# First projection to pooling as one stage, and attention units ordered by query tile

## The reference

```python
h = rmsnorm(x, norm1_w)
p = h @ w_in                                   # 1024 -> 20 blocks of 128 channels
p_rw = p + mu[0] * (prev - p) + mu[1] * (nxt - p)   # token shift, 16 of the blocks
r, k, v, wd, ad, gd = split(p_rw)
kk = heads(k * k_k); kk = kk / max(sqrt(sum(kk * kk)), 1e-12)
g = sigmoid(gd) @ g_up
for d in range(2):                             # both directions of time
    wlog = -softplus(-(w0[d] + tanh(wd[d]) @ w_up[d])) - 0.5
    decay = exp(-exp(wlog)); a = sigmoid(a0[d] + ad[d] @ a_up[d])
    kd = k * (1 + (a - 1) * k_a)
    o += wkv7_scan(r, decay, kd, v, kk, a, reverse=(d == 1))
    bonus += sum(r * kd * r_k) * v
y_pool = multiscale_pool(p_pool, pool_w, pool_scale)   # windows 2, 4, 8, 16
...
s = einsum('bnqhd,bnkhd->bnhqk', q, k) * 64 ** -0.5 + bias   # 8 heads of mixer A, 8 of B
o = einsum('bnhqk,bnkhd->bnqhd', softmax(s), v)
```

## Time and profile before

| | |
|---|---|
| median of 3 runs | 3314.09 us (3310.55 to 3316.93) |
| the profiled execution | 3311.4 us, of which the span of instructions 3309.2 us |
| TensorE busy | 2833.8 us, 86% |
| VectorE busy | 1845.0 us, 56% |
| ScalarE busy | 1138.4 us, 34% |
| GpSimd busy | 733.5 us, 22% |
| mean granted TensorE clock | 0.949 |

### The profile page before, as it was taken

One profiled execution on the slowest core, in us unless ns is written; L12 is line 12 of the kernel. 1 busy time (PEld: TensorE's weight loads), 2 busy tenths in 40 slices (PEclk: granted clock), 3 DMA queues, 4 the chain that ended last, 5 costly groups with the idle time before them and its releaser, 6 DMA issues. The chain is left out here.

```text
span 3309.2 us, 44276 instructions
## 1 busy us (share of the span) xinstructions
PE 2833.8 (86%) x15630; PEld 1842.2 (56%) x15630; DVE 1845.0 (56%) x3559; ACT 1138.4 (34%) x2659; POOL 733.5 (22%) x594
## 2 busy tenths in 40 slices
PE   8839996987778787877887787998989999999988
PEld 6509995763223233322332224887866776778876
DVE  6673346576676666666664545444256643464422
ACT  3422322224344343434343343222125444332211
POOL 0030000025444554545455551000010000000000
PEclk9859998999999999999999998999999999999999
DMA  3111002349999999999999994323221111232231
GB/s 127 43 60 35 3 3 72 99 179 420 404 405 399 420 415 416 401 420 419 415 407 420 420 421 191 95 94 116 71 96 58 52 58 45 83 96 95 89 123 43
DMA packets 114869, 680.51 MB, mean 206 GB/s; under 512 B 12584, under 2 KB 16552, under 8 KB 46632
## 3 DMA queue, kind: packets, MB, share of 16 engines
q0 software_dynamic: 73728, 536.90, 39.4%
q1 hardware_dynamic: 41000, 141.68, 13.1%
HBM read 673.29 MB, written 7.86 MB: 206 GB/s over the span
## 5 line engine op out<-in xcount | busy, mean ns | idle before, releaser
L1384 PE MATMUL expert_total<-uv_rows,h 128*128 128x512 f32 x2048 | 1009.1, 633 | 268.4 <-ACT h L1479 262.9
L1663 DVE CUSTOM_DVE_ANT_0 uv_rows<-uv_rows,h_tok 128x1024 f32<-128x1024 f32 x512 | 621.6, 1225 | 482.6 <-DMA uv_rows<-in_peer_uv,expert_ids 479.8
L1384 PEld LDWEIGHTS expert_total<-uv_rows,h 128*128 128x128 f32 x2048 | 380.1, 198 | 893.6 <-issue 545.4
L1325 POOL DMA_INDIRECT uv_rows<-in_peer_uv,expert_ids x512 | 647.9, 1265 | 627.3 <-PE expert_total L1384 522.0
L1474 ACT ACTIVATE expert_acts<-expert_dots 128x1 f32<-128x1 f32 x512 | 103.7, 203 | 682.4 <-DVE expert_dots L1663 678.0
L261 PE MATMUL ffn_in_out<-ffn_h_hi,ffn_in_w_hi 128*128 128x512 f32 x704 | 281.3, 400 | 14.9 <-DVE ffn_in_w_lo L346 14.9
L263 PE MATMUL ffn_in_out<-ffn_h_hi,ffn_in_w_lo 128*128 128x512 f32 x704 | 279.8, 397 | 0.0
L262 PE MATMUL ffn_in_out<-ffn_h_lo,ffn_in_w_hi 128*128 128x512 f32 x704 | 279.8, 397 | 0.0
L338 DVE TENSOR_TENSOR ffn_in_w_lo<-ffn_in_w,ffn_in_w_hi 128x1024 fp32r<-128x1024 f32 x86 | 105.4, 1225 | 213.6 <-ACT ffn_in_w_hi L289 213.5
L1479 ACT ACTIVATE h<-const_sb,expert_weights 128x128 f32<-128x128 f32 x512 | 205.5, 401 | 16.7
L289 ACT CAST ffn_in_w_hi<-ffn_in_w 128x1024 fp32r<-128x1024 f32 x86 | 90.1, 1048 | 262.1 <-PE ffn_in_out L263 255.0
(11 more groups left out here) (409 smaller groups left out, 4221.0 us busy)
## 6 DMA issues: line engine op xcount, KB each, us to landing
ffn_in_w<-in_ffn_w_in SPq DMA_DIRECT2D x86, 512.0 KB, 3.5
mix_w<-in_w_in SPq DMA_DIRECT2D x39, 512.0 KB, 3.5
ffn_out_w<-in_ffn_w_out SPq DMA_DIRECT2D x14, 1408.0 KB, 6.2
w_in_w<-in_w_in SPq DMA_DIRECT2D x19, 512.0 KB, 3.5
uv_rows<-in_peer_uv,expert_ids POOLq DMA_INDIRECT x512
wq_w<-in_peer_wq SPq DMA_DIRECT2D x15, 512.0 KB, 3.5
w_out_w<-in_w_out SPq DMA_DIRECT2D x14, 512.0 KB, 3.6
branches_w<-in_w_branches SPq DMA_DIRECT2D x15, 256.0 KB, 2.7
```

The costliest lines, as they stand in the source:

```text
L1325: nc.gpsimd.indirect_dma_start(out=uv[:, first + j].rearrange("p a d -> p (a d)"), out_offset=None, in_=uv_tab, in_offset=bass.IndirectOff ...
L1384: mm = nc.tensor.matmul(total[:, t % 2, half], diag[:, b], v[:, b, half * T:(half + 1) * T], start=False, stop=False)
L1663: a.tensor_tensor_reduce(out=u[:, b], in0=u[:, b], in1=h_tok[:, t], scale=1.0, scalar=0.0, op0=ALU.mult, op1=ALU.add, accum_out=dot[:, b:b ...
```

## The change

`front` takes the place of the first projection, `rwkv_operands` and `gate_bonus_pool`. It walks 23 steps: steps 0 to 19 have the products of one block each, in the order `ORDER1`, and every engine's queue has between them the small work that the tables name for the step, written out by hand. In one step TensorE's order is: products, key sums, spread, lora, gate, pooling, bonus. ScalarE's is: wait for the products of the step, `high(n + 2)`, first half of a shift (`middle`), key parts, root, tanh, gate sigmoid, sigmoids, gate copy, pooling copy, exponentials. VectorE's is: wait for the products, `low(n + 2)`, evacuation, inversion of the key norms, `kk`, `behind`, `scan`, keys, rates, term, sums of the pooling, bonus, shift. The evacuation goes through two banks, and blocks 2 and 3 through banks of the lora products. In detail:

- The key norms of all pairs are written into one bank at 32 partitions each, so one root, one maximum and one reciprocal serve for all four, and four products of 32 rows (`head_spread`) spread them again.
- VectorE's difference of scan and sigmoid is gone: ScalarE takes the exponential from the scan shifted by one token (with ones set beforehand). The affine key factor and the copies to `w_end` go from VectorE to ScalarE. Large copies of v and of the pooling input are gone.
- The pooling's mean uses a constant factor and corrects eight tokens at each end (four small instructions).
- Gate and pooling are stored block by block by ScalarE's queue, the bonus by SP.
- Constants (`head_spread`, `inv_counts`, `lora`, `pool_w`, `g_up`) are fetched in SP's queue between weight blocks 2 to 6.

In `mixer_in` a pair's units are ordered by query tile, the longest first, with both heads of a tile next to each other; the groups have 2, 2 and 4 units instead of 3, 3 and 2; `weigh` takes both heads of a tile and alternates between them per key tile; `pT` has four buffers instead of three.

```diff
+ORDER1 = [B_K + 0, B_K + 1, B_POOL + 0, B_WD, B_K + 2, B_K + 3, B_AD, B_R + 0, B_GD, B_GD + 1,
+          B_R + 1, B_POOL + 1, B_POOL + 2, B_V + 0, B_V + 1, B_R + 2, B_V + 2, B_R + 3, B_POOL + 3, B_V + 3]
+TENSOR_KK = {7: (0, 1), 8: (2, 3)}
+TENSOR_LORA = {8: (0,), 11: (1,), 13: (2,), 17: (3,)}
+TENSOR_GATE = {12: (0,), 14: (1, 2, 3)}
+TENSOR_MIX = {6: (0,), 14: (1,), 18: (2,), 20: (3,)}
+TENSOR_BONUS = {22: (0, 1, 2, 3)}
+SCALAR_MIDDLE = {2: (0, 1), 3: (3,), 4: (4,), 5: (5,), 7: (6, 7), 9: (8,), 10: (9, 10), 14: (13,), 15: (14,), 16: (15,), 18: (16,), 22: (17, 19)}
+SCALAR_KK = {3: (0,), 5: (1,), 7: (2, 3)}
+SCALAR_SIGMOIDS = {8: (0,), 11: (1,), 13: (2,), 19: (3,)}
+SCALAR_EXPS = {9: (0,), 12: (1,), 14: (2,), 20: (3,)}
+SCALAR_GATE = {11: (0,), 13: (1,), 14: (2,), 15: (3,)}
+SCALAR_MIX = {5: (0,), 15: (1,), 19: (2,), 22: (3,)}
+VECTOR_SHIFT = {2: (0,), 3: (1, 3), 4: (4,), 6: (5,), 7: (6, 7), 9: (8, 9), 13: (10,), 14: (13,), 15: (14,), 16: (15,), 17: (16,), 19: (17,), 21: (19,)}
+VECTOR_SCAN = {8: (0,), 11: (1,), 14: (2,), 17: (3,)}
+VECTOR_KEYS = {9: (0,), 11: (1,), 13: (2,), 18: (3,)}
+VECTOR_RATES = {9: (0,), 12: (1,), 13: (2,), 17: (3,)}
+VECTOR_BEHIND = {10: (0,), 13: (1,), 16: (2,), 20: (3,)}
+VECTOR_TERM = {12: (0,), 15: (1,), 21: (2, 3)}
+VECTOR_SUMS = {4: (0,), 11: (1,), 14: (2,), 18: (3,)}
+VECTOR_BONUS = {20: (0, 1), 22: (2, 3)}
+TENSOR_SPREAD, SCALAR_ROOT, SCALAR_TANH, SCALAR_GATE_SIGMOID = 9, 8, 4, 10
+VECTOR_INVERT, VECTOR_KK = 8, 9
+N_FRONT = N_IN1 + 3
...
+            for n in range(SLOT, N_IN1):
+                sp.wait_ge(parted, n - SLOT + 1)
+                sp.dma_start(raw[:, n % SLOT], source(n)).then_inc(w_in[n % SLOT], 16)
...
+                if n:
+                    pe.wait_ge(parted, n + 1)
+                if n >= 4:
+                    pe.wait_ge(free, n - 1)
...
+            def kk_sum(i):
+                pe.wait_ge(kk_squares, i + 1)
+                rows = slice(32 * i, 32 * i + 32)
+                bank = two_bank("kk", 0) if i else two_free("kk", 0)
+                nc.tensor.matmul(bank[rows], consts("heads")[:, 48:80], kk_sq[:, i % 2], start=True, stop=True
+                                 ).then_inc(kk_summed, 1)
...
+                for i in range(PAIRS):
+                    rows = slice(32 * i, 32 * i + 32)
+                    nc.tensor.matmul(za[:, i // 2, i % 2], sel[rows, :], inv[rows, :], start=True, stop=True).then_inc(kk_spread, 1)
...
+                cols = slice(i * P, (i + 1) * P)
+                for d in range(2):
+                    rows = slice(HEAD * d, HEAD * d + HEAD)
+                    for a in range(2):
+                        nc.tensor.matmul(za[:, d, a], lora[rows, a, cols], WA[rows, a], start=True, stop=True).then_inc(zs, 1)
...
+            def middle(n):
+                b = ORDER1[n]
+                act.wait_ge(free, n + 1)
+                if b == B_V:
+                    act.wait_ge(gates, PAIRS)
+                if b == B_V + 2:
+                    act.wait_ge(gate_stored[0], 16 * PAIRS // 2)
+                if b == B_V + 3:
+                    act.wait_ge(mixed, 4)
+                nc.scalar.activation(place(b), p[:, SHIFTS[n] % 2, 1:T + 1], ACT.Copy, scale=rest[:, b:b + 1]).then_inc(rested, 1)
...
+            def exponentials(i):
+                for d in range(2):
+                    to, by = (slice(1, CHUNK), slice(0, CHUNK - 1)) if d == 0 else (slice(0, CHUNK - 1), slice(1, CHUNK))
+                    act.wait_ge(cums, 2 * i + d + 1)
+                    if i:
+                        act.wait_ge(by_pool, 2 * i - 1 + d)
+                    nc.scalar.activation(wt[:, d], cum[:, d], ACT.Exp, scale=-DECAY).then_inc(exped_once, 1)
+                    nc.scalar.activation(by_chunk(ar[:, d, 0, i])[:, :, to], by_chunk(cum[:, d])[:, :, by], ACT.Exp, scale=-DECAY
+                                         ).then_inc(exped_once, 1)
+                for d in range(2):
+                    act.wait_ge(exped_once, 4 * i + 2 * d + 2)
+                    nc.scalar.activation(cum[:, d], cum[:, d], ACT.Exp, scale=DECAY)
+                    ends = wt[:, d, CHUNK - 1::CHUNK] if d == 0 else wt[:, d, 0::CHUNK]
+                    nc.scalar.copy(w_end[:, d, :, i:i + 1].rearrange("p c a -> p (c a)"), ends).then_inc(exps, 1)
...
+            def take_gate(i):
+                act.wait_ge(gates, i + 1)
+                if i >= 2:
+                    act.wait_ge(gate_stored[i % 2], 16 * (i // 2))
+                nc.scalar.copy(gate[i % 2], two_bank("gate", i)).then_inc(gate_made, 1)
+                act.wait_ge(gate_made, i + 1)
+                act.dma_start(gate_dram[:, i], gate[i % 2]).then_inc(gate_stored[i % 2], 16)
...
+            for n in range(N_FRONT):
+                if n < N_IN1:
+                    act.wait_ge(done, n + 1)
+                    if n + SLOT < N_IN1:
+                        high(n + SLOT)
...
+            def scan(i):
+                for d in range(2):
+                    way = slice(None) if d == 0 else slice(None, None, -1)
+                    if i:
+                        dve.wait_ge(operands, 2 * i - 1 + d)
+                    dve.wait_ge(sigs, 4 * i + 2 * d + 1)
+                    a.tensor_tensor_scan(out=cum[:, d, way], data0=consts("reset"), data1=ar[:, d, 1, i, way], initial=0.0,
+                                         op0=ALU.mult, op1=ALU.add).then_inc(cums, 1)
...
+            def behind(i):
+                dve.wait_ge(keys_scaled, 2 * i + 2)
+                a.tensor_tensor(K[:, i], bk[:, 0, 1, i], bk[:, 1, 1, i], ALU.add).then_inc(kds, 1)
+                for d in range(2):
+                    dve.wait_ge(exps, 2 * i + d + 1)
+                    dve.wait_ge(rates_scaled, 2 * i + d + 1)
+                    a.scalar_tensor_tensor(out=bk[:, d, 0, i], in0=bk[:, d, 0, i], scalar=-1.0, in1=cum[:, d],
+                                           op0=ALU.mult, op1=ALU.mult)
+                    dve.wait_ge(kds, i + 1)
+                    a.tensor_tensor(bk[:, d, 1, i], bk[:, d, 1, i], cum[:, d], ALU.mult).then_inc(operands, 1)
...
-HEADS_AT = [(hh, t) for hh in range(2) for t in range(TT)]
+HEADS_AT = [(hh, t) for t in reversed(range(TT)) for hh in range(2)]
 NU = len(HEADS_AT)
 UNITS = [(i, hh, t) for i in range(2 * PAIRS) for hh, t in HEADS_AT]
-GROUP_AT = {(A_FIRST if i < PAIRS else B_FIRST - 3 * PAIRS) + 3 * i + g: range(i * NU + (0, 3, 6)[g], i * NU + (3, 6, 8)[g])
+GROUP_AT = {(A_FIRST if i < PAIRS else B_FIRST - 3 * PAIRS) + 3 * i + g: range(i * NU + (0, 2, 4)[g], i * NU + (2, 4, 8)[g])
             for i in range(2 * PAIRS) for g in range(3)}
 NONE = range(0)
 PROBS = 6
-S_RING, T_RING = 3, 2
+S_RING, T_RING, P_RING = 3, 2, 4
...
-                i, hh, t = UNITS[u]
-                rows = slice(HEAD * hh, HEAD * hh + HEAD)
+                i, _, t = UNITS[u]
                 if u % NU == 0:
                     if i:
                         pe.wait_ge(stored, i)
                     pe.wait_ge(taken, T_USE["turn", 9 + 3 * i if i < PAIRS else 20] + 1)
-                pe.wait_ge(taken, T_USE["unit", u] + 1)
+                pe.wait_ge(taken, T_USE["unit", u + 1] + 1)
                 for j in range(t + 1):
-                    v = pr[:, C_VA + i if i < PAIRS else C_VB, j * P + HEAD * hh:j * P + HEAD * hh + HEAD]
-                    mm = nc.tensor.matmul(o_ps[rows, t * P:(t + 1) * P], v, pT[:, u % S_RING, j * P:(j + 1) * P],
-                                          start=(j == 0), stop=(j == t))
-                mm.then_inc(weighed, 1)
+                    for hh in range(2):
+                        rows = slice(HEAD * hh, HEAD * hh + HEAD)
+                        v = pr[:, C_VA + i if i < PAIRS else C_VB, j * P + HEAD * hh:j * P + HEAD * hh + HEAD]
+                        mm = nc.tensor.matmul(o_ps[rows, t * P:(t + 1) * P], v, pT[:, (u + hh) % P_RING, j * P:(j + 1) * P],
+                                              start=(j == 0), stop=(j == t))
+                        if j == t:
+                            mm.then_inc(weighed, 1)
             def between(n):
                 if n in TURNS_AT:
...
-                for u in GROUP_AT.get(n - 1, NONE):
+                for u in GROUP_AT.get(n - 1, NONE)[::2]:
                     weigh(u)
...
-                if u >= S_RING:
-                    act.wait_ge(weighed, u - S_RING + 1)
-                nc.scalar.copy(pT[:, u % S_RING, 0:keys_of(t)], t_bank("unit", u)[:, 0:keys_of(t)]).then_inc(taken, 1)
+                if u >= P_RING:
+                    act.wait_ge(weighed, u - P_RING + 1)
+                nc.scalar.copy(pT[:, u % P_RING, 0:keys_of(t)], t_bank("unit", u)[:, 0:keys_of(t)]).then_inc(taken, 1)
...
-            with nc.sbuf_tensor("p_in", [P, N_IN1, T], F32) as q:
-                with ExitStack() as s0:
-                    h = parts(nc, s0, "h1", KD)
-                    norm = Norm(nc, s0, "norm1", x, vec("norm1"), consts("ones"), RMS_EPS1,
-                                sq=ar[:, 0].rearrange("p a b t -> p (a b) t"),
```

(75 more changed lines are left out.)

584 lines of the change are left out of this document (343 added, 241 removed).

## The result

| | before | after |
|---|---|---|
| median of the runs | 3314.9 us | 3227.5 us (3222.7 to 3232.5, 4 runs) |
| ratio | | 0.9738 (95%: 0.9720 to 0.9756) |
| span of the profiled execution | 3309.2 us | 3230.7 us |
| first product of the recurrence | 249.65 us | 183.94 us |
| mixer, first product to the first of the branches | 371.2 us | 353.5 us |

The forecast was 3234 us (range 3216 to 3256). The front gave 65.7 us where 58 were expected, the attention 17.7 where 22 were. The stage of the table's last row was not edited; it gives back 3.6 us. The spans fall by 78.5 us, the medians by 87.4: the profiled execution of the changed kernel was the slowest of its four (3232.5 us).

A forecast was written before the change was run, and what follows sets the result against it. TensorE was taken to bound the first projection and attention, VectorE and half-clock chains the 121 us between projection and recurrence. Profiled 3311.4 minus 58 and 22 gives 3231.4, plus 2.7 to the median: 3234 us, range 3216 to 3256.

The forecast's parts named there:

- The front: Three opening stages merged into one: recurrence begins at 191.5 instead of 249.65 us, -58, bounds -67 and -40.
- the attention: Reordered units in the attention stage: 2.8 us saved in each of eight pairs, -22, bounds -6 and -28.
- Block 8's end: In the front, block 8's products end at 68.5 us: 67.2 less 1.8 saved waiting plus 3.1 of added products.
- Steps 9 to 19: Front's main stretch: TensorE's own work 85.4 us, VectorE's queue 76.9, block 19 ending at 157, bounds 154 and 170.
- The tail: Front's work after block 19: 31 us to the last write at 188, hidden behind nothing; bounds 25 and 36.
- The `S_RING` wait: Attention's group of four: the fourth score product waits for the first one's bank, 0.4 to 0.7 us, taken 0.55.
- the softmax chain's cover: Attention steps: cover shrinks from about 9.5 to 8.6 us; if gone, each group loses what it gained.
- The rule on the tiling mode: Tiling changes drain TensorE: front gains about a dozen edges, 2.5 us in the sum, 8 more if each empties a product.
- (a): Front's queues block one another: TensorE waits 1.5 us more at each of steps 9 to 19; 3254 us, chance 0.14.
- (b): Attention's column halves don't pair in full, so weighing saves nothing: +16, 3250 us, chance 0.06.
- (c): New pauses bring TensorE to 1.2 GHz in steps 8 to 19, its 85 us becoming 170; 3320 us, chance 0.03.
- (d): Better than the sum: waits vanish and the tail's half-clock products run fast; 3220 us, chance 0.07.

The follow-up runs named there:

- e6: Changed kernel with eight of GpSimd's sixteen front products left out and the other eight on 8 of 512 columns, results not the reference's: 3219.5 us, one run.
- the attention alone: The kernel before, with its three old opening stages, given only the new order of attention units: 3294.2 us, ratio 0.9941.
- e3: Changed kernel with each pair of units weighed one head after the other instead of alternating: 3229.2 us, ratio 0.9743.
- The repeat: The changed kernel without an edit, run again beside later experiments: 3230.0 us, ratio 0.9754.
- e1: Changed kernel with the attention units, groups, weighing and three pT buffers of the kernel before, so only the front is new: 3246.7 us, ratio 0.9804.
- e4: Changed kernel with ScalarE's four sigmoids of pair 3 in its step 17 instead of 19: 3219.4 us, ratio 0.9721.
- e5: Changed kernel with the scores of the last two units of each group of four made two eighths of a block later: 3222.4 us, ratio 0.9730.

## Why the prediction was right

**The total was partly luck.** By the spans the time fell by 78.5 us where 80 had been worked out, but the front gave 7.7 more, the attention 4.3 less, the expert stage, for which the sum had nothing, took 3.6 back, and the other stages without an edit 1.3.

**The front, -65.7 instead of -58.** The mechanism was right: TensorE bounds steps 9 to 19, and a tail of VectorE's work follows. Three terms were too large by 7.6 in all:
- *Block 8's end* came at 65.8, not 68.5. The two key sums cost 0.5 each and not 0.85 (their records start under 0.01 us apart: the two write different groups of 32 output partitions and run side by side), and the pooling product 0.95: 1.2 less with the changes of form. The other 1.5 lie in the first blocks, where besides the wait at 39.08 the one for the second block shrank from 1.31 to 0.36 us; the remainder I didn't trace.
- *Steps 9 to 19* took 86.75 us, with 4.0 of waiting and thus 82.7 of its own work, where 88.5 had been taken and 85.4 was the bare work. The lora groups took 2.6 less: 1.9 to 2.0 each, the lower bound, not 2.6. The argument that the order would cost the overlap rested on a misreading: the group of the earlier trace rows was made in the same order. The four gate products took 8.3 and not 6.8, since the second part of each, with only 32 rows, costs as much as the first (1.05 us), and the stretch at half clock cost 1.6. Key sums, spread, pooling products and changes of form make up the rest. The two waits were of the foreseen size but one in another place: not for a low part at step 17 but for an evacuation behind VectorE's two shift pairs of step 9, at 90.4 us.
- *The tail* took 27.75 us, not 31. The table load, 1.28, was priced in it but had been done in ScalarE's idle time; the last bonus product and its two writes took 2.4, not 3.3. The way to the recurrence was 3.65 us, taken as 3.6. The other 1.2 I didn't trace. The stall was 10.98 us long, not some 8.

VectorE ended `low(19)` 76.2 us after block 8's end and reached its stall at 142.56 us, after 76.8. 76.9 had been worked out, but as two errors that cancel: 69.5 us of work (GpSimd costs half as much here, `e6`) and 7.2 of waiting for high parts, which the sum didn't have.

**The attention, -17.7 instead of -22.** Per pair, 1.8 had been taken for weighing, 1.0 for the scores and nothing for turning. Weighing gave 1.77, as in the sum. The scores gave 0.63 in the second half and 0.30 in the first, because the group of four took 1.7 to 1.8 us there and 2.04 in the first half, not 1.46. Turning gave 0.57 in the second half (3.72 us before, 3.15 now), which the sum didn't have, and nothing in the first. So a pair lost 2.94 us, close to the 2.8 as two errors that cancel, and 2.07 in the first half. The pairs alone sum to 4 x 2.94 + 4 x 2.07 = 20.0, minus 1.6 for the stretch at half clock is 18.4. The 22.1 of the attention alone are no proof of the 22: they are about these 20.0 and the 2.5 us saved before the first weighing (99.4 less 96.9), of which 1.6 are the stretch at half clock that it lacks there. The `S_RING` wait was the one warned of, and named as a sign of being wrong although 0.55 of it was in the sum; the softmax chain's cover was never gone.

**The rule on the tiling mode.** The edges show as a distance of 0.32 us between the last product and the weighing and of 0.34 behind the next product, where products otherwise follow each other every 0.23: about 0.1 us an edge. The Trainium skill, "TensorEngine Tiling (Array Packing)", Key Properties, says that a change of the tiling mode drains TensorE; the trace agrees that an edge costs something, but shows no emptied product of 0.85 us at any of those that I looked at.

**The shared port.** GpSimd's multiplies beside VectorE's took 1.71 and VectorE's 1.75 us, each alone 1.3 and 0.69. The Trainium skill, "SBUF — State Buffer", "SBUF: two separate sides", has the two engines share one pair of ports as an exclusive lock for a whole instruction when VectorE's has two inputs in SBUF and GpSimd's reads SBUF; the trace agrees roughly: a VectorE instruction and a multiply together take 1.68 us (169.85 less 168.17), where one after the other would be 0.60 + 1.25 = 1.85 and side by side 1.25.

**The rivals.** (a) Queues blocking one another: TensorE waited 4.0 us in steps 9 to 19, not 16 more. (b) Halves that don't pair: refuted by `e3`, though the gain of pairing is half of what I put on the series. (c) The clock: 0.98 from 66 to 153 us, so this rival is out by size. But it did fall there, to 0.50 behind the wait of 2.6 us, for 1.6 us lost, which the prediction had named as a sign of being wrong. The repeat has such a stretch at 121 us instead, behind the wait of 1.4 us, and `e1`, `e4` and `e5` have both. With the same front the recurrence begins at 183.9 to 185.0 in the kernels with one such stretch and at 185.5 in the two with both. (d) Better than the sum: the total came near it (3227.5 against 3220), but not by its reason. Waits didn't vanish, and the last two bonus products still ran at 0.50 (3.78 us from 175.78).

**The unedited expert stage** gave back 3.6 us. It takes 1315.8 to 1323.3 us in the nine kernels, without a pattern: nothing in the prediction covers it, and its spread of 7 us is as large as most differences between these kernels.

## What to carry to other kernels

When a stage bound by one engine stands beside a stage bound by another, merging them can hide at most the shorter one. Here 121 us stood between the projection and the recurrence, and 65.7 were gained: 31 us of tail and way stayed, and the projection became 24 us longer by the small products, the waits and the clock. The price lies in the written queues, so walk each engine's order and look for an instruction that waits for one standing later in another's queue. Such a stall is not worth its full length when mended (11 us became 6.7), because the next late one is close behind and the neighbours in the queues slow each other. When two kernels differ by under 10 us, compare them stage by stage before the total, since an unedited stage can move by as much.

## What the runs showed of the hardware

- TensorE products of 128 rows and 64 columns, alternating between column halves: 8 in 1.02 us, one half after the other 1.51 us.
- Four plain f32 products of 64 rows and 512 columns, two of one row half and then two of the other, take 1.9 to 2.0 us: the halves run side by side in this order.
- Two plain f32 products with 32 columns of weights each, into different groups of 32 output partitions, take 0.98 us together, one product with 128 columns of weights 0.95; a product of only 32 rows takes 1.05 (each for 512 tokens, at full clock).
- ScalarE's table load runs ahead of the wait of the instruction that needs it: it was done 4.3 us before.
- A VectorE instruction of 512 columns with two inputs in SBUF takes 0.69 us, and 1.75 beside a multiply of GpSimd; over steps 9 to 19 the price was 0.57 us of VectorE's time per multiply, in the tail's full queue 1.04.
- The granted clock can fall to 0.50 for 3 us in the middle of a busy stage, which costs 1.6 us. In the mixer's pairs three profiles show it, behind TensorE's waits of 0.44 and 0.74 us, and two with the same waits don't; at the mixer's second block the eight profiles with a wait of 2.6 to 2.7 us show it, and the two with a wait of 1.8 and 2.0 don't.
